# A diffusion trunk on one core: the feature-major projections stream 128 context and 512 latent tokens per weight tile, where they streamed 320 and 320

## The chip, the core and the metric

The kernel runs on one core of a Trainium2 chip. The metric is the device time of one execution in microseconds. The engines are named as in the profile: PE is TensorE's matmul (PEld its weight loads), ACT is ScalarE, DVE is VectorE, POOL is GpSimd and SP is SyncE, which here only issues the loads of the weight stream.

## The reference: one step of a two-layer trunk over 640 tokens

There are 128 context tokens and 512 latent tokens with 1024 features. Layer 0 mixes tokens by retention (4 heads, key width 256, value width 512, forward and backward), layer 1 by windowed attention (16 query heads, 4 key heads, width 64). Each mixer is followed by a gated feed-forward part whose input projection has 5632 outputs and is followed by a convolution of width 3 along the tokens. Context and latent tokens share all weights, but they have their own modulation, and the convolution does not cross from one to the other:

```
def conv_ffn(h, w_in, conv_w, conv_b, w_out):
    a = h @ w_in
    ap = jnp.pad(a, ((0, 0), (1, 1), (0, 0)))
    a = ap[:, :L] * conv_w[0] + ap[:, 1:L + 1] * conv_w[1] + ap[:, 2:] * conv_w[2] + conv_b
    u, g = jnp.split(a, 2, axis=-1)
    return (jax.nn.silu(g) * u) @ w_out
...
    xc = xc + mc[5] * conv_ffn(hc, ...)      # context, 128 tokens
    xl = xl + ml[5] * conv_ffn(hl, ...)      # latent, 512 tokens
```

Everything is in float32.

## The kernel before, in words

**Numbers as two parts.** A float32 operand of a large projection is split into a high part and the rest, both of type fp32r (`w_h`, `w_l` for weights, `h_h`, `h_l` for the normalised tokens, `m_h`, `m_l` for the feed-forward's middle, `y_h`, `y_l` for retention's output). A product is three matmuls, high by high, low by high and high by low, which add up in one PSUM bank. Each matmul instruction brings its own load of the 128x128 stationary operand.

**Weights.** SP streams chunks of 128x1024 into four raw slots. ACT writes `w_h` of a chunk (line 717) and POOL `w_l` (line 1009) into a ring of two. PE's wait for a chunk stands at the head of each tile (`weights`).

**Three kinds of projection on PE.**

- `feature_tile` (lines 335 and 344): the weight tile is stationary and the tokens move, so that the output is 128 features by 640 tokens. The 640 tokens are more than a PSUM bank of 512 float32 holds, so a tile uses two banks, `banks` and `banks + 1`, with half the tokens each, `HALF` = 320. A tile is 2 halves x 8 slices of the 1024 features x 3 products = 48 matmuls. There are 114 such tiles: 4 for each of 4 heads (queries and keys), 44 in the first projection of each feed-forward, and 10 in attention (queries and keys). In 104 of them (line 344) one half runs through all slices and then the other. In 10 of them (line 335), those with a `norm` argument, the halves alternate within a slice, three matmuls each. Four of those ten are the first after a norm and start each slice when its `h_l` is there; the other six have the same code within a loop.
- `token_chunk` (line 359): the tokens are stationary and 512 (in one place 256) weight columns move.
- `out_proj` (line 383): the weights are stationary and 320 tokens move. It takes its tokens by the slice `lo_hi` too.

**Who reads the banks.** After a feature tile ACT copies it out of PSUM. Context and latent tokens go to different places, because the convolution pads between them and rotary embedding is for latent tokens only. With halves of 320 the first bank holds 128 context tokens and 192 latent ones (`CUT` = 192), so three copies are made: 128, 192 and 320 columns (lines 801 to 803, 896 to 898 and 937 to 944). Then DVE works on the copy (the convolution from line 1291 on). PE's next tile but one into the same banks waits for the last of the copies.

**Order.** All engines run hand-written programs with semaphores. There is no scheduler. PE works through: adaptive-norm weights and first norm, four heads (feature tiles, output projection of the head before, token chunks, scores, retention steps), first feed-forward in three groups, attention, second feed-forward in three groups, final norm.

Of the kernel before, what the change touches and what calls it, by code (L numbers as in the profile page):

```python
# [20 lines left out]
ACT = mybir.ActivationFunctionType  # L21
# [5 lines left out]
NCTX, NLAT = 128, 512  # L27
T = NCTX + NLAT
TT = T // P
HALF = T // 2  # L30
CUT = HALF - NCTX
# [109 lines left out]
def build(nc, dr):  # L141
    with ExitStack() as ctx:
# [6 lines left out]
        ps = ctx.enter_context(nc.psum_tensor("ps", [P, 8, 512], F32))  # L149
# [62 lines left out]
        lat_in = front[:, 0:4 * NLAT].rearrange("p (b t) -> p b t", b=4)  # L212
# [50 lines left out]
        def lo_hi(b):  # L263

            return slice(b * HALF, b * HALF + HALF)
# [12 lines left out]
        def ada_at(b, g, q, i):  # L278
# [2 lines left out]
                return None  # L281
            return 12 + q + 2 * i if g == 0 else 20 + i

        def out_bank(mh, at):

            return (at + 4) % 8 if mh == 0 else at
# [27 lines left out]
        def _(pe):  # L314
# [7 lines left out]
            def feature_tile(b, j, i, banks, free, norm=None):  # L322

                s = weights(b, j, i)
                if norm is not None:
                    free(0)
                    free(1)
                    for k in range(KT):  # L330
                        wait_rest(pe, norm, k)
                        wh, wl = (w[:, s, k * P:(k + 1) * P] for w in (w_h, w_l))
                        for half in range(2):
                            for n, (w, x) in enumerate(((wh, h_h), (wh, h_l), (wl, h_h))):
                                mm = nc.tensor.matmul(ps[:, banks + half, 0:HALF], w, x[:, k, lo_hi(half)],  # L335
                                                      start=(k == 0 and n == 0), stop=(k == KT - 1 and n == 2))
                    mm.then_inc(chunk_done, 1)
                    return
                for half in range(2):
                    free(half)  # L340
                    for k in range(KT):
                        wh, wl = (w[:, s, k * P:(k + 1) * P] for w in (w_h, w_l))
                        for n, (w, x) in enumerate(((wh, h_h), (wh, h_l), (wl, h_h))):
                            mm = nc.tensor.matmul(ps[:, banks + half, 0:HALF], w, x[:, k, lo_hi(half)],  # L344
                                                  start=(k == 0 and n == 0), stop=(k == KT - 1 and n == 2))
                mm.then_inc(chunk_done, 1)

# [274 lines left out]
            b = SEG["att"]  # L622
# [84 lines left out]
        def _(act):  # L707
# [86 lines left out]
            def head(b, h, first_head):  # L794
                for j in range(4):
                    act.wait_ge(chunk_done, b.done(j, h))
                    hi(b, j + 2, h)
                    bank, scale = 2 * (j % 2), 1.0 if j < 2 else DK ** -0.5
                    ctx_to = (qT if j < 2 else kT)[:, j % 2, 0:NCTX]
                    lat = front[:, j * NLAT:(j + 1) * NLAT]  # L800
                    nc.scalar.activation(ctx_to, ps[:, bank, 0:NCTX], ACT.Copy, scale=scale)
                    nc.scalar.activation(lat[:, 0:CUT], ps[:, bank, NCTX:HALF], ACT.Copy, scale=scale)
                    nc.scalar.activation(lat[:, CUT:NLAT], ps[:, bank + 1, 0:HALF], ACT.Copy,  # L803
                                         scale=scale).then_inc(qk_evac, 1)
                    if j == 0:
                        act.dma_start(S[:], dr["state"][h]).then_inc(S_in, 16)
                    if not first_head and j in (1, 2):
                        turn_y(h - 1, (0, 1, 2) if j == 1 else (3, 4))
                j = 4
                if not first_head:  # L810
                    for k in range(4):
                        hi(b, 4 + k + 2, h)
                    j = 8
                for proj in range(3):
                    for kc in range(3):
                        hi(b, j + kc + 2, h)
                    for t in range(TT):
                        if t == TT - 1:
                            act.wait_ge(chunk_done, b.done(j + 3, h))
                        else:  # L820
                            act.wait_ge(tile_done, 12 * h + 4 * proj + t + 1)
                        if proj == 0:
                            if t == 0:
                                act.wait_ge(rope_done, 2 * h + 2)
                            op = nc.scalar.copy(v[:, t, :], ps[:, t, :])
                        else:
                            op = nc.scalar.activation((gf, gb)[proj - 1][:, t, :], ps[:, t, :], ACT.Silu)
                        op.then_inc(tok_evac, 1)
                    hi(b, j + 3 + 2, h)
                    j += 4  # L830
                    if proj == 0:

                        act.wait_ge(scores_done, h + 1)
                        if first_head:
                            act.wait_ge(dec_ready, 1)
                        zf, zb = zeta[:, 0, bass.ds(h, 1)], zeta[:, 1, bass.ds(h, 1)]
                        pair = lambda bank: ps[:, bank, :].rearrange("p (c d) -> p c d", c=2)
                        nc.scalar.activation(kz[:, 0, 0, :], ps[:, 6, P:P + DK], ACT.Copy, scale=zf)
                        nc.scalar.activation(kz[:, 1, 0, :], ps[:, 6, P:P + DK], ACT.Copy, scale=zb)
                        nc.scalar.activation(kz[:, 0, 1:3, :], pair(7), ACT.Copy, scale=zf)  # L840
                        nc.scalar.activation(kz[:, 1, 1, :], ps[:, 7, DK:2 * DK], ACT.Copy, scale=zb)
                        nc.scalar.activation(kz[:, 0, 3, :], ps[:, 4, 0:DK], ACT.Copy, scale=zf)
                        nc.scalar.activation(kz[:, 1, 2:4, :], pair(4), ACT.Copy, scale=zb).then_inc(kz_done, 1)

                for n in range(10):
                    act.drain()
                    act.wait_ge(o_done, 10 * h + n + 1)
                    nc.scalar.activation(junk[:], ps[:, 6 + n % 2, :], ACT.Square,
                                         accum_out=small[:, 64 + n:65 + n]).then_inc(ss_done, 1)
                    if n == 1:  # L850
                        if not first_head:
                            act.wait_ge(st_stored, 32 * h)
                        for d in range(2):
                            act.wait_ge(u_done, 8 * h + d + 1)
                            nc.scalar.copy(st_out[:, d], ps[:, 2 * d:2 * d + 2, :]).then_inc(st_copied, 1)
                        for d in range(2):
                            act.wait_ge(st_copied, 2 * h + d + 1)
                            act.dma_start(dr["new_state"][d, h], st_out[:, d]).then_inc(st_stored, 16)
# [21 lines left out]
            def ffn_phase(l, norm):  # L880
                tiles0 = 0
                for g, tiles in enumerate(GROUPS):
                    b = SEG["in", l, g]
                    pairs = b.mains // 2
                    with act.Fori(0, tiles // pairs) as i:
                        for q in range(pairs):
# [3 lines left out]
                            for w in range(2):  # L890
                                act.wait_ge(chunk_done, b.done(2 * q + w, i))
                                hi(b, 2 * q + w + 2, i)

                                act.wait_ge(conv_done[l], 2 * n + w + 1 + 2 * pairs * i)
                                a = ca[:, par, w]
                                nc.scalar.copy(a[:, 1:1 + NCTX], ps[:, 2 * w, 0:NCTX])
                                nc.scalar.copy(a[:, NCTX + 2:NCTX + 2 + CUT], ps[:, 2 * w, NCTX:HALF])
                                nc.scalar.copy(a[:, NCTX + 2 + CUT:NCTX + 2 + NLAT],  # L898
                                               ps[:, 2 * w + 1, 0:HALF]).then_inc(a_evac[l], 1)
                                if blk is not None and w == 0:  # L900
                                    slot, used = b.chunk(b.ada[(4 * q if g == 0 else 0) + 3], i)
                                    act.wait_ge(raw_used[slot], used)
                                    nc.scalar.copy(ada_o[:, q, :], ps[:, 4 + q, :]).then_inc(ada_copied, 1)
# [24 lines left out]
            for j in range(10):  # L928
# [10 lines left out]
                else:  # L939
                    for r in range(2):  # L940
                        rows = slice(64 * r, 64 * r + 64)
                        nc.scalar.copy(ak[rows, 2 * (j - 8) + r, 0:NCTX], ps[rows, bank, 0:NCTX])
                nc.scalar.copy(lat_in[:, j % 4, 0:CUT], ps[:, bank, NCTX:HALF])
                nc.scalar.copy(lat_in[:, j % 4, CUT:NLAT], ps[:, bank + 1, 0:HALF]).then_inc(aqk_evac, 1)
            hi(b, 12, 0)
            for t in range(TT):
                if t == TT - 1:
# [594 lines left out]
```

## Time and profile before

| | us |
|---|---|
| median of two runs | 2219.54 (2217.85 and 2221.23) |
| span of the profiled execution, the only time given of it | 2220.6 |
| PE busy | 2100.9 (95%) |
| PEld busy | 1833.4 (83%) |
| DVE busy | 920.7 (41%) |
| POOL busy | 665.6 (30%) |
| ACT busy | 634.8 (29%) |

The page lists the busy time of each engine, the span in 40 slices, the chain of work that ended last and the costliest groups of instructions. A matmul's duration in a row is from its start to its modelled end. Matmuls overlap, so that the time from one start to the next, which I call the pace, is shorter: it comes from a stretch of the chain or of the timeline divided by the number of instructions in it. A group's line in the chain counts instructions, and a float32 matmul (not fp32r) appears as two instructions.

### The profile page before, as it was taken

The numbers are of one execution on the slowest core, as the hardware profiler recorded it, in microseconds if no ns is written. First come the engines' busy times: TensorE is split into PE (matmuls) and PEld (weight loads), VectorE is DVE, ScalarE is ACT, GpSimd is POOL, SyncE is SP. The second block draws the span as 40 slices with busy tenths as digits, with TensorE's granted clock in tenths as the row PEclk, the third lists the DMA queues.
The fourth block names the chain that finished last, engine by engine and source line by source line (L and its number), as shares of the span: only waits on it lengthen the run. The fifth ranks groups of instructions, "written<-read, shape, count | busy, mean of one in ns | idle before, by whom it ended". The sixth has DMA issues, their size and how long they took to land.

```text
span 2220.6 us, 32261 instructions
## 1 busy us (share of the span) xinstructions
PE 2100.9 (95%) x12352; PEld 1833.4 (83%) x12352; DVE 920.7 (41%) x1452; ACT 634.8 (29%) x1222; POOL 665.6 (30%) x404
## 2 busy tenths in 40 slices
PE   5799999999999997999999998899989899999997
PEld 3686888598598766899999997885559899999997
DVE  1511420340241036552553363646742764364363
ACT  2323212212222323331232232234432332232232
POOL 1323233233323323233333334330004233333333
PEclk7799999999999997999999998899989899999998
DMA  6422232232133202552343222120001122222221
GB/s 242 165 69 76 95 105 76 95 106 75 58 106 104 94 20 76 176 200 79 110 139 112 73 72 81 49 72 1 1 9 59 48 76 76 76 76 76 73 71 56
DMA packets 52435, 189.94 MB, mean 86 GB/s; under 512 B 5872, under 2 KB 7152, under 8 KB 51696
## 3 DMA queue, kind: packets, MB, share of 16 engines
q1 hardware_dynamic: 47232, 171.99, 24.0%
q10 hardware_dynamic: 5104, 16.53, 1.9%
q8 instruction: 75, 1.23, 0.2%
q14 instruction: 24, 0.20, 0.0%
HBM read 181.41 MB, written 7.08 MB: 85 GB/s over the span
## 4 chain that ended last, share of the span: by engine, by line
PE 86%; DVE 5%; issue 2%; ACT 1%; POOLq 1%; DMA 1%; POOL 1%; DVEq 1%; ACTq 0%; SPq 0%
PE ps L344 33%; PE ps L383 20%; PE ps L359 16%; PE ps L335 2%; PE ps L399 2%; PE ps L684 2%; PE ps L528 2%; PE ps L537 1%; PE ps L650 1%; DVE front L1120 1%; POOLq L1035 1%; PE ps L667 1%; DVE front L1115 1%; PE ps L523 1%; PE ps L419 1%
## 5 line engine op out<-in xcount | busy, mean ns | idle before, releaser
L1009 POOL TENSOR_TENSOR w_l<-raw,w_h 128x1024 fp32r<-128x1024 f32 x232 | 560.7, 2417 | 1362.4 <-ACT w_h L717 1361.9
L344 PE MATMUL ps<-h_h,w_h 128*128 128x320 f32 x1664 | 518.3, 311 | 2.0 <-issue 2.0
L344 PE MATMUL ps<-h_l,w_h 128*128 128x320 f32 x1664 | 514.9, 309 | 0.0
L344 PE MATMUL ps<-h_h,w_l 128*128 128x320 f32 x1664 | 514.8, 309 | 0.0
L717 ACT CAST w_h<-raw 128x1024 fp32r<-128x1024 f32 x232 | 243.3, 1049 | 930.3 <-PE ps L383 307.5
L344 PEld LDWEIGHTS ps<-h_h,w_h 128*128 128x128 f32 x1664 | 313.2, 188 | 17.3 <-issue 17.3
L344 PEld LDWEIGHTS ps<-h_l,w_h 128*128 128x128 f32 x1664 | 313.1, 188 | 0.2 <-issue 0.2
L344 PEld LDWEIGHTS ps<-h_h,w_l 128*128 128x128 f32 x1664 | 313.0, 188 | 0.0
L1291 DVE TENSOR_SCALAR cc<-ca,vec 128x641 f32<-128x641 f32 x88 | 165.1, 1876 | 181.8 <-ACT ca L898 181.4
L1155 DVE SCALAR_TENSOR_TENSOR xT<-ps,mods,xT 128x128 f32<-128x128 f32 (+2 forms) x264 | 107.9, 437 | 305.7 <-PE ps L383 305.7
L383 PE MATMUL ps<-m_h,w_h 128*128 128x320 f32 x704 | 217.9, 310 | 2.3 <-DVE mods L1141 2.3
L383 PE MATMUL ps<-m_h,w_l 128*128 128x320 f32 x704 | 217.7, 309 | 0.0
L383 PE MATMUL ps<-m_l,w_h 128*128 128x320 f32 x704 | 217.7, 309 | 0.0
L359 PE MATMUL ps<-w_h,h_h 128*128 128x512 f32 (+1 forms) x520 | 200.2, 385 | 4.9 <-ACT front L803 4.9
L359 PE MATMUL ps<-w_h,h_l 128*128 128x512 f32 (+1 forms) x520 | 198.9, 383 | 0.0
L359 PE MATMUL ps<-w_l,h_h 128*128 128x512 f32 (+1 forms) x520 | 198.8, 382 | 0.0
L383 PEld LDWEIGHTS ps<-m_h,w_h 128*128 128x128 f32 x704 | 132.6, 188 | 2.5 <-DVE mods L1141 2.5
L383 PEld LDWEIGHTS ps<-m_l,w_h 128*128 128x128 f32 x704 | 132.7, 189 | 0.0
L383 PEld LDWEIGHTS ps<-m_h,w_l 128*128 128x128 f32 x704 | 132.6, 188 | 0.0
L359 PEld LDWEIGHTS ps<-w_h,h_h 128*128 128x128 f32 x520 | 98.3, 189 | 26.7 <-ACT front L803 5.8
L359 PEld LDWEIGHTS ps<-w_h,h_l 128*128 128x128 f32 x520 | 98.2, 189 | 19.1
L359 PEld LDWEIGHTS ps<-w_l,h_h 128*128 128x128 f32 x520 | 98.3, 189 | 18.6
(187 smaller groups left out, 2853.2 us busy)
## 6 DMA issues: line engine op xcount, KB each, us to landing
raw<-stream_dram SPq DMA_DIRECT2D x328, 512.0 KB, 3.5
S<-state_dram ACTq DMA_DIRECT2D x4, 1024.0 KB, 7.0
new_state_dram<-st_out ACTq DMA_DIRECT2D x8, 512.0 KB, 3.8
xT<-x_dram ACTq DMA_DIRECT2D x1, 2560.0 KB, 11.7
y_dram<-aq ACTq DMA_DIRECT2D x8, 320.0 KB, 2.4
dm<-diff_dram ACTq DMA_DIRECT2D x1, 512.0 KB, 4.1
rope_t<-rope_t_dram ACTq DMA_DIRECT2D x1, 512.0 KB, 6.7
rope_a<-rope_a_dram ACTq DMA_DIRECT2D x1, 512.0 KB, 3.5
```

The source lines that it names most:

```text
L335: mm = nc.tensor.matmul(ps[:, banks + half, 0:HALF], w, x[:, k, lo_hi(half)], start=(k == 0 and n == 0), stop=(k == KT - 1 and n == 2))
L344: mm = nc.tensor.matmul(ps[:, banks + half, 0:HALF], w, x[:, k, lo_hi(half)], start=(k == 0 and n == 0), stop=(k == KT - 1 and n == 2))
L359: mm = nc.tensor.matmul(ps[:, bank(t), 0:n_cols], x[:, k, t * P:(t + 1) * P], w, start=(k == 0 and n == 0), stop=(k == KT - 1 and n == 2))
L383: mm = nc.tensor.matmul(ps[:, bank, 0:HALF], w, x[:, k, lo_hi(half)], start=(k == 0 and n == 0), stop=(k == tiles - 1 and n == 2))
L399: mm = nc.tensor.matmul(ps[32 * g:32 * g + 32, 4 + par, :], csil[:, k, :], raw[:, s, kk * 512:(kk + 1) * 512], start=(k < 4), stop=(k >= 4))
L419: mm = nc.tensor.matmul(ms_ps[:, t:t + 1], src[:, t * P:(t + 1) * P], ones[:, 0:1], start=(k == KT - 3), stop=(k == KT - 1))
L528: mm = nc.tensor.matmul(ps[:, 6 + d, :], q[:, t, c * P:(c + 1) * P], S[:, d, t, :], start=False, stop=(t == 1))
L684: mm = nc.tensor.matmul(ps[64 * (kv % 2):64 * (kv % 2) + 64, 7, :], val[:, kv * HD:(kv + 1) * HD], pT[:, u % 2, kb, :], start=(kb == 0), s ...
L717: nc.scalar.copy(w_h[:, r, :], raw[:, s, :]).then_inc(hi_ready[r], 1)
L1009: nc.gpsimd.tensor_tensor(w_l[:, r, :], raw[:, s, :], w_h[:, r, :].bitcast(F32), ALU.subtract).then_inc(raw_used[s], 1)
L1155: op = V.scalar_tensor_tensor(out=xT[:, m, tok], in0=ps[:, bank, cols], scalar=mods[:, l, 8 * gate + m, s:s + 1], in1=xT[:, m, tok], op0=A ...
L1291: V.tensor_scalar(c, a[:, 1:1 + CONV], tap[1], tap[3], ALU.mult, ALU.add)
```

## The change

The slice of tokens that a feature tile's two halves take is no longer 0 to 320 and 320 to 640, but 0 to 128 (the context) and 128 to 640 (the latent tokens). The number of matmuls, their order, their weights and the banks stay; each pair of 320 columns becomes one matmul of 128 columns and one of 512. ACT's copies fall from three per tile to two, of 128 and 512 columns. `token_chunk` and `out_proj` are untouched.

```diff
+        def ctx_lat(b):
+
+            return (slice(0, NCTX), slice(NCTX, T))[b]
...
                         for half in range(2):
                             for n, (w, x) in enumerate(((wh, h_h), (wh, h_l), (wl, h_h))):
-                                mm = nc.tensor.matmul(ps[:, banks + half, 0:HALF], w, x[:, k, lo_hi(half)],
+                                mm = nc.tensor.matmul(ps[:, banks + half, 0:(NCTX, NLAT)[half]], w,
+                                                      x[:, k, ctx_lat(half)],
                                                       start=(k == 0 and n == 0), stop=(k == KT - 1 and n == 2))
...
                         for n, (w, x) in enumerate(((wh, h_h), (wh, h_l), (wl, h_h))):
-                            mm = nc.tensor.matmul(ps[:, banks + half, 0:HALF], w, x[:, k, lo_hi(half)],
+                            mm = nc.tensor.matmul(ps[:, banks + half, 0:(NCTX, NLAT)[half]], w,
+                                                  x[:, k, ctx_lat(half)],
                                                   start=(k == 0 and n == 0), stop=(k == KT - 1 and n == 2))
...
                     nc.scalar.activation(ctx_to, ps[:, bank, 0:NCTX], ACT.Copy, scale=scale)
-                    nc.scalar.activation(lat[:, 0:CUT], ps[:, bank, NCTX:HALF], ACT.Copy, scale=scale)
-                    nc.scalar.activation(lat[:, CUT:NLAT], ps[:, bank + 1, 0:HALF], ACT.Copy,
-                                         scale=scale).then_inc(qk_evac, 1)
+                    nc.scalar.activation(lat, ps[:, bank + 1, :], ACT.Copy, scale=scale).then_inc(qk_evac, 1)
...
                                 nc.scalar.copy(a[:, 1:1 + NCTX], ps[:, 2 * w, 0:NCTX])
-                                nc.scalar.copy(a[:, NCTX + 2:NCTX + 2 + CUT], ps[:, 2 * w, NCTX:HALF])
-                                nc.scalar.copy(a[:, NCTX + 2 + CUT:NCTX + 2 + NLAT],
-                                               ps[:, 2 * w + 1, 0:HALF]).then_inc(a_evac[l], 1)
+                                nc.scalar.copy(a[:, NCTX + 2:NCTX + 2 + NLAT], ps[:, 2 * w + 1, :]).then_inc(a_evac[l], 1)
...
-                nc.scalar.copy(lat_in[:, j % 4, 0:CUT], ps[:, bank, NCTX:HALF])
-                nc.scalar.copy(lat_in[:, j % 4, CUT:NLAT], ps[:, bank + 1, 0:HALF]).then_inc(aqk_evac, 1)
+                nc.scalar.copy(lat_in[:, j % 4, :], ps[:, bank + 1, :]).then_inc(aqk_evac, 1)
```

## Rows read from the trace of the kernel before

**Rows 1.** The page: span, busy time and granted clock.

```profile
span 2220.6 us, 32261 instructions
...
PE 2100.9 (95%) x12352; PEld 1833.4 (83%) x12352; DVE 920.7 (41%) x1452; ACT 634.8 (29%) x1222; POOL 665.6 (30%) x404
...
PEclk7799999999999997999999998899989899999998
```

**Rows 2.** The page: the chain that ended last, by engine and by line.

```profile
PE 86%; DVE 5%; issue 2%; ACT 1%; POOLq 1%; DMA 1%; POOL 1%; DVEq 1%; ACTq 0%; SPq 0%
PE ps L344 33%; PE ps L383 20%; PE ps L359 16%; PE ps L335 2%; PE ps L399 2%; PE ps L684 2%; PE ps L528 2%; PE ps L537 1%; PE ps L650 1%; DVE front L1120 1%; POOLq L1035 1%; PE ps L667 1%; DVE front L1115 1%; PE ps L523 1%; PE ps L419 1%
```

**Rows 3.** Chain by time, second feed-forward: start us, us, what xcount.

```profile
1906.52 112.64 PE ps L344 x768
```

**Rows 4.** The same, retention: 512 moving columns.

```profile
144.69 54.45 PE ps L359 x240
```

**Rows 5.** The same, attention's values: 256 moving columns.

```profile
1470.52 14.41 PE ps L359 x120
```

**Rows 6.** PE groups by line and form: xcount | busy us, mean ns.

```profile
L335 PE MATMUL ps<-h_h,w_h 128*128 128x320 f32 x160 | 61.0, 381 | 42.1 <-DVE h_l L1125 36.3 <-POOL h_l L1041 5.7
...
L497 PE MATMUL ps<-qT,kT 128*128 128x128 f32 x80 | 10.0, 280 | 2.8 <-ACT front L825 2.8
```

**Rows 7.** The same on PEld, the weight loads.

```profile
L344 PEld LDWEIGHTS ps<-h_l,w_h 128*128 128x128 f32 x1664 | 313.1, 188 | 0.2 <-issue 0.2
...
L650 PEld LDWEIGHTS ps<-ak,aq 128*128 128x128 f32 x128 | 19.4, 192 | 0.0
...
L425 PEld LDWEIGHTS ps<-front,cst 128*128 128x128 f32 x50 | 11.3, 326 | 8.5 <-DVE front L1098 8.5
...
L656 PEld LDWEIGHTS ps<-maskb,identb 128*128 128x128 bf16 x48 | 4.7, 98 | 7.6 <-issue 7.2
```

**Rows 8.** Timeline of PEld in a norm sum: start us, us, what.

```profile
1372.08 1.42 PEld L419 LDWEIGHTS ps<-cst,front 128*128 128x128 f32 x12
```

**Rows 9.** Timeline of PEld, a little later in the same sum.

```profile
1374.26 1.40 PEld L419 LDWEIGHTS ps<-cst,front 128*128 128x128 f32 x6
```

**Rows 10.** Windows around Rows 8, around Rows 9 and in Rows 3.

```profile
core 0: us, PE busy (x) PEld busy (x) DVE busy (x) ACT busy (x) POOL busy (x), PEclk, DMA share, GB/s
1372.20:1373.40 1.20, 1.20 (x13) 1.20 (x12) 0.00 (x0) 0.00 (x0) 0.00 (x0) 1.00 0.00 0
1374.50:1375.50 1.00, 1.00 (x6) 1.00 (x6) 0.00 (x0) 0.00 (x0) 0.00 (x0) 0.50 0.00 0
1906.50:2019.00 112.50, 112.50 (x770) 112.50 (x769) 66.33 (x67) 37.05 (x75) 38.55 (x16) 1.00 0.23 71
```

**Rows 11.** Timeline of PE, retention's scores: float32, 128 moving columns.

```profile
706.55 1.73 PE L497 MATMUL ps<-qT,kT 128*128 128x128 f32 x14
```

**Rows 12.** Timeline of PE, attention's masks: bf16, 128 moving columns.

```profile
1533.04 0.22 PE L653 MATMUL ps<-maskb,identb 128*128 128x128 bf16 x1
1533.10 0.22 PE L656 MATMUL ps<-maskb,identb 128*128 128x128 bf16 x1
```

**Rows 13.** Timeline of PE in the first feature tile after the first norm.

```profile
65.62 0.47 PE L335 MATMUL ps<-h_l,w_h 128*128 128x320 f32 x1
65.89 0.47 PE L335 MATMUL ps<-h_h,w_l 128*128 128x320 f32 x1
...
69.76 0.63 PE L335 MATMUL ps<-h_h,w_h 128*128 128x320 f32 x1 [0.92 <-DVE h_l L1125]
```

**Rows 14.** Groups on ACT and who waits, on DVE: columns as in Rows 6.

```profile
L898 ACT COPY ca<-ps 128x320 f32<-128x320 f32 x88 | 38.8, 441 | 0.0
...
L897 ACT COPY ca<-ps 128x192 f32<-128x192 f32 x88 | 28.5, 324 | 0.0
...
L984 ACT COPY pT<-ps 128x512 f32<-128x512 f32 x32 | 17.1, 594 | 0.0
...
L1291 DVE TENSOR_SCALAR cc<-ca,vec 128x641 f32<-128x641 f32 x88 | 165.1, 1876 | 181.8 <-ACT ca L898 181.4 <-issue 0.2
```

## The prediction, made before the change was run

> **What bounds the kernel now.** I read the page first. PE is busy for 95% of the span and no other engine for more than 41%, weight loads apart [rows 1]. PE carries 86% of the chain that ended last, and line 344, the feature tile, 33% of it, more than any other line [rows 2]. So what a matmul of a feature tile costs is paid in full, unless PE would have waited there anyway.
>
> The view to read next is the chain in order of time, because a matmul's duration overlaps its neighbour's and only the pace counts. In the second feed-forward 768 matmuls of 320 columns follow each other in one piece of 112.64 us: 146.7 ns each [rows 3]. With 512 moving columns, also fp32r with a load each, the pace is 54.45/240 = 226.9 ns [rows 4], and with 256 it is 14.41/120 = 120.1 ns [rows 5]. All of it is at the full granted clock, 2.4 GHz [rows 1, 10]. The three points lie on one line: (226.9 - 146.7)/192 = 0.418 ns per column, which is a column per clock, and (146.7 - 120.1)/64 = 0.416. What is left is 226.9 - 512/2.4 = 13.6, 13.4 and 13.4 ns per matmul. If nothing else counted, 128 columns would take 53.3 + 13.4 = 66.7 ns, a pair 66.7 + 226.9 = 293.6 ns, and the pair of before is 2 x 146.7 = 293.4 ns. The split would then be free. The question is whether the line goes on below 256 columns.
>
> **Why I think it does not.** Under each matmul lies the load of the next stationary operand, and a shorter matmul hides less of it. The trace shows how fast loads can follow each other when the matmuls are next to nothing. In the norm's sum one column moves per load: twelve loads in 1.42 us [rows 8], of which the last lasts about 0.19 as other float32 loads do [rows 7], so (1.42 - 0.19)/11 = 112 ns each, at a granted clock of 1.00 [rows 10]. These are float32 loads, though. The fp32r loads of the feature tiles last 188 ns in their rows, those of bf16 98, and those of float32 192 [rows 7]. A fp32r load therefore looks like a float32 one and not like a bf16 one. In the scores, float32 with 128 moving columns, fourteen matmuls take 1.73 us [rows 11], the last of them 0.28 [rows 6], so (1.73 - 0.28)/13 = 112 ns. So neither of these two streams of 4-byte loads goes faster than 112 ns at the full clock. The bf16 masks follow each other at 1533.10 - 1533.04 = 0.06 us with 128 columns [rows 12], so it is the load and not the matmul that makes the floor.
>
> The Trainium skill bears on this in two places. The page "TensorE: Matmul & The Clock Gate", section "LDWEIGHTS (loading the stationary operand)", gives the stationary columns over 1.2 GHz, 107 ns for 128; by that the sum below would be 107 us in place of 131, an estimate. The same page's section "Weight-path perf modes — Fast Weight Load (FWL) and DoubleRow" keeps the fast load to types that are not FP32, and the trace agrees as to bf16 against float32 (98 against 192 ns); on which side fp32r stands only the 188 ns say.
>
> **The change, part by part.**
>
> - *Moving columns of the first half, 320 to 128.* Bounds: 112 ns from the float32 loads [rows 8], and 120.1 ns from the nearest row of the same kind of matmul, 256 columns of fp32r [rows 5], if the 13.4 ns come on top of a load of 107 as they come on top of the columns. I take 116, the middle, since each of the rows is like the new matmul in one respect. Against 146.7 that is -30.7 ns. Below 112 I leave 107 as the end, 256 columns' time at a column per clock, since the 256-column matmul hides its load too [rows 5]. Above 120 I leave 140, in case a load can begin only when the matmul before it has begun, and its own matmul waits longer for it than the columns take; the present pace of 147 ns would hide anything up to that.
> - *Moving columns of the second half, 320 to 512.* 226.9 against 146.7 ns: +80.2 ns [rows 3, 4]. Weights are stationary here and tokens in rows 4, but both are 128x128 fp32r against 512 columns of fp32r.
> - *Per tile.* 24 x (-30.7 + 80.2) = 24 x 49.5 ns = 1.19 us. That is 7.04 us (48 x 146.7) grown to 8.23. In the ten tiles whose halves alternate, each 128-column matmul still covers one load, and each 512-column one as well, so the same sum holds.
> - *Tiles in which PE waits anyway.* Line 335 has 42.1 us of idle time before it, nearly all for `h_l` [rows 6]. It lies in four tiles, the first ones after a norm. There a step of two slices takes 69.76 - 65.19 us, that is 4.57, of which PE waits 0.92 [rows 13]. The clock is at half there: the pace is 65.89 - 65.62 = 0.27 us [rows 13], 320 columns at 1.2 GHz. Twelve matmuls become 6 x 0.22 + 6 x 0.43 = 3.9 us in place of 3.2 to 3.65, still under 4.57. The last slice is paid. So 4 x 7/8 = 3.5 tiles are hidden behind DVE's norm, and 110.5 of 114 count. If that cover were gone, it would cost 3.5 x 1.19 = 4 us more.
> - *ACT's copies.* 192 and 320 columns take 324 and 441 ns in their rows, 512 take 594 [rows 14]. Two overlapping starts become one, at most 0.17 us per tile less. DVE waits 181.4 us for these copies in 85 waits [rows 14], but PE doesn't wait for DVE within the phases: the piece of 112.64 us has no gap [rows 3]. Only at the ends of six feed-forward groups is it on the path: under 1 us in all. I put nothing. The wait of PE for the copies (two tiles back) only gets longer cover.
> - *Banks.* PE writes 512 columns into a bank that ACT empties before PE comes back to it a tile later. A longer tile makes this looser. POOL, SP and the DMA queues have the same work and more time for it.
>
> **Sum.** 110.5 x 1.19 = 131 us. The profiled execution's span is 2220.6 us, so I expect a span of 2352. The median of the runs shown is 1.1 us below that span, so the time is **2351 us**. With 107 ns as pace it is 110.5 x 24 x 40.5 ns = 107 us, 2327; with 120.1 it is 110.5 x 24 x 53.6 = 142 us, 2362; with 140 it is 110.5 x 24 x 73.5 = 195 us, 2414.
>
> **The rivals.**
>
> *The load does not bind: not slower.* If a fp32r load can be as quick as bf16's, or two loads can be under way, the line goes on to 66.7 ns and the change costs 0.2 ns per pair: 2220 us. For it: bf16 goes at 60 ns with 128 columns [rows 12], and a 188 ns load beside a 120.1 ns pace [rows 5, 7] shows that loads already overlap. Against it: the 112 ns of rows 8 and of rows 11. The point where it decides: 2% are 44.4 us, 44.4/(110.5 x 24) = 16.7 ns, so a pace under 66.5 + 16.7 = 83 ns is no measurable change. The Trainium skill speaks for this one: "TensorE: Matmul & The Clock Gate", section "Back-to-back issue gap", gives about 81 ns per matmul for a sustained stream of load and matmul pairs at 128 columns, by which the estimate is 38 us, 2258; no row of this trace with 4-byte loads is near 81. I give it 9%, of which 1% for faster.
>
> *A short fp32r matmul loses its single pass.* If 128 columns were handled as float32, a matmul would cost two instructions of 112 ns [rows 11], 223 ns: 24 x (223 - 146.7 + 80.2) = 3.76 us per tile, +415 us, 2635. For it: nothing in the trace shows fp32r below 256 columns. Against it: the line is straight from 512 down to 256 columns [rows 3 to 5], with no sign of a threshold. 7%.
>
> *The clock falls.* Within the first half of a tile the array would work 53 of 116 ns for 2.8 us. In the norm's sum, with one column per load, the granted clock went from 1.00 to 0.50 after some 2 us, and the loads then follow at (1.40 - 0.33)/5 = 214 ns [rows 8 to 10], if the last lasts 0.33 as line 425's do [rows 7]. Every tenth of the tiles' 909 us of work that ran at half clock would add 91 us: 2442, and half of it some 2800. Against it: there the array had next to no columns, while here 128 of them move and 5.4 us of full work follow in every tile, and attention has streams of 128 columns at clock 9 of the page's digits [rows 1]. 6%.
>
> **The numbers.** The forecast has 78%, the four cases together 100%. The range runs from the 107 ns end to the 140 ns end, 2325 to 2415, and holds the forecast's 78% and the mildest part of the falling clock, some 2%. Two per cent, about what a measurement tells from no change here, are 44 us. Faster by that: 1%; within: 8%; slower: 91%, all the rest.
>
> **What would show it.** In the profile after: the pace of 128-column stretches of line 349 (24 in a row) near 116 ns, each 24 in 2.8 us; of 512 columns 227 ns; tiles of 8.2 us in the chain, 16 tiles in 132 us where 112.64 stood; PEld durations near 190 in both; the other two kinds of projection at their old pace; and the granted clock in 40 slices as before, stretched. A pace of 67 ns proves the first rival, of about 220 the second, and digits of 5 to 8 in the feed-forward's slices the third. The forecast is wrong also if a PE wait appears between tiles, which I see no source for.

## The result: 2351.4 us, 5.9% slower

The changed kernel takes 2351.4 us (2350.35 and 2352.45), against 2219.54 before. The ratio is 1.0588 with a 95% interval of 1.057 to 1.0605. The profiled execution's span is 2350.7 us, 130.1 more than before.

The page after, first its span, busy times and granted clock, then who made up the chain. The line numbers move by a few: 344 is now 349, 335 is 339, 383 is 389.

```profile
span 2350.7 us, 32147 instructions
...
PE 2238.0 (95%) x12352; PEld 1849.2 (79%) x12352; DVE 922.3 (39%) x1452; ACT 628.3 (27%) x1108; POOL 658.9 (28%) x404
...
PEclk7799999999999989999999997999987999999998
```

```profile
PE 88%; DVE 4%; issue 2%; ACT 1%; POOLq 1%; POOL 1%; DMA 1%; DVEq 1%; ACTq 0%; SPq 0%
PE ps L349 37%; PE ps L389 19%; PE ps L365 15%; PE ps L339 3%; PE ps L405 2%; PE ps L690 2%; PE ps L534 2%; PE ps L543 1%; PE ps L656 1%; DVE front L1121 1%; POOLq L1036 1%; PE ps L673 1%; PE ps L425 1%; PE ps L529 1%; DVE front L1116 1%
```

Against [rows 1] PE is busy 137 us more, and the other engines as before within 7 us (PEld 16). Against [rows 2] the feature tile's share grew from 33% to 37% and the other projections kept their time (19% of 2351 is 20% of 2221). The digits of the granted clock are the same kind of row, stretched.

The chain in order of time says what a tile costs now. The columns are start in us, us, and what, with the number of instructions.

```profile
239.60 8.14 PE ps L349 x48
...
432.55 10.00 PE ps L349 x48
...
1820.25 28.09 PE ps L349 x144
...
1856.55 24.54 PE ps L349 x144
...
1946.60 56.32 PE ps L389 x384
2002.92 130.85 PE ps L349 x768
```

The piece of 16 tiles that took 112.64 us [rows 3] takes 130.85: 8.18 us per tile in place of 7.04. The output projection beside it has 56.32/384 = 146.7 ns as before the change. The first piece is the first tile of head 1, the second the same tile of head 2, and the two pieces of x144 are three tiles each near the start of the second feed-forward. I come back to these four.

How the tile divides is read from PE's timeline, one row per matmul.

```profile
2100.88 0.22 PE L349 MATMUL ps<-h_h,w_h 128*128 128x128 f32 x1
2100.94 0.28 PE L349 MATMUL ps<-h_l,w_h 128*128 128x128 f32 x1
2101.05 0.27 PE L349 MATMUL ps<-h_h,w_l 128*128 128x128 f32 x1
...
2103.40 0.28 PE L349 MATMUL ps<-h_h,w_l 128*128 128x128 f32 x1
2103.51 0.45 PE L349 MATMUL ps<-h_h,w_h 128*128 128x512 f32 x1
2103.80 0.40 PE L349 MATMUL ps<-h_l,w_h 128*128 128x512 f32 x1
2104.04 0.40 PE L349 MATMUL ps<-h_h,w_l 128*128 128x512 f32 x1
...
2106.34 0.39 PE L349 MATMUL ps<-h_h,w_h 128*128 128x512 f32 x1
2106.57 0.39 PE L349 MATMUL ps<-h_l,w_h 128*128 128x512 f32 x1
```

From 2101.05 to 2103.40 there are 21 steps of 128 columns: 112 ns each. A fp32r matmul of 128 columns after another thus goes at the pace of the float32 loads of [rows 8], and 45 ns slower than its columns and 13.4 ns would take. From 2106.34 on, 512 columns take 0.23 us as in [rows 4]. Two things at the seams are worth seeing. The first short matmul is followed after 0.06 us, and the first long one makes up for it and is followed only after 0.29 us. Together they take 0.35 us, and 112 + 227 = 339 ns is what a short and a long one cost elsewhere: nothing is gained. Why the two records divide the time so unevenly is not shown. And the long matmuls after the seam take 0.24 and 0.23 us; in the trace it is some ten of them at 232 ns on average, until the 227 ns are back. That lag is 0.05 us per tile.

By groups, PE's two forms of line 349 and the wait before the first tiles:

```profile
L349 PE MATMUL ps<-h_h,w_h 128*128 128x512 f32 x832 | 333.4, 401 | 0.0
...
L349 PE MATMUL ps<-h_l,w_h 128*128 128x128 f32 x832 | 230.3, 277 | 0.0
...
L339 PE MATMUL ps<-h_h,w_h 128*128 128x128 f32 x80 | 22.9, 286 | 36.1 <-DVE h_l L1126 31.4 <-POOL h_l L1042 4.7
```

and the loads, on PEld:

```profile
L349 PEld LDWEIGHTS ps<-h_l,w_h 128*128 128x128 f32 x1664 | 318.6, 191 | 33.2 <-issue 0.2
...
L389 PEld LDWEIGHTS ps<-m_l,w_h 128*128 128x128 f32 x704 | 132.0, 187 | 0.2
```

A fp32r load now lasts 191 ns on average where the feature tiles had 188 [rows 7], and 187 still under 320 columns. The load durations alone tell next to nothing of the change; it is the pace that tells.

ACT's copy of 512 columns, and DVE's wait for it:

```profile
L901 ACT COPY ca<-ps 128x512 f32<-128x512 f32 x88 | 52.0, 591 | 0.0
...
L1292 DVE TENSOR_SCALAR cc<-ca,vec 128x641 f32<-128x641 f32 x88 | 166.5, 1892 | 276.1 <-ACT ca L901 276.1
```

DVE waits 276.1 us for ACT where it waited 181.4 [rows 14]. That is 95 us more waiting on an engine off the path: PE delivers later. The chain's stretch of 16 tiles has no wait of PE for DVE in it.

### The profile page after: what moved, and what is told of

Same layout as the page of the kernel before. It is cut to its first block, busy times and chain, and to the rows that moved or that the text cites. A ratio compares the mean times of both kernels' runs of the same rounds, so it can differ in the third digit from the quotient of the medians.

```text
span 2350.7 us, 32147 instructions
## 1 busy us (share of the span) xinstructions
PE 2238.0 (95%) x12352; PEld 1849.2 (79%) x12352; DVE 922.3 (39%) x1452; ACT 628.3 (27%) x1108; POOL 658.9 (28%) x404
## 3 DMA queue, kind: packets, MB, share of 16 engines
HBM read 181.41 MB, written 7.08 MB: 80 GB/s over the span
## 4 chain that ended last, share of the span: by engine, by line
PE 88%; DVE 4%; issue 2%; ACT 1%; POOLq 1%; POOL 1%; DMA 1%; DVEq 1%; ACTq 0%; SPq 0%
PE ps L349 37%; PE ps L389 19%; PE ps L365 15%; PE ps L339 3%; PE ps L405 2%; PE ps L690 2%; PE ps L534 2%; PE ps L543 1%; PE ps L656 1%; DVE front L1121 1%; POOLq L1036 1%; PE ps L673 1%; PE ps L425 1%; PE ps L529 1%; DVE front L1116 1%
## 5 line engine op out<-in xcount | busy, mean ns | idle before, releaser
L1010 POOL TENSOR_TENSOR w_l<-raw,w_h 128x1024 fp32r<-128x1024 f32 x232 | 554.2, 2389 | 1497.1 <-ACT w_h L723 1496.6
L349 PE MATMUL ps<-h_h,w_h 128*128 128x128 f32 (+1 forms) x1664 | 561.2, 337 | 2.2 <-issue 2.2
L349 PE MATMUL ps<-h_h,w_l 128*128 128x128 f32 (+1 forms) x1664 | 557.2, 335 | 0.0
L349 PE MATMUL ps<-h_l,w_h 128*128 128x128 f32 (+1 forms) x1664 | 555.9, 334 | 0.0
L349 PEld LDWEIGHTS ps<-h_h,w_h 128*128 128x128 f32 x1664 | 318.5, 191 | 50.0 <-issue 17.7
L349 PEld LDWEIGHTS ps<-h_h,w_l 128*128 128x128 f32 x1664 | 318.2, 191 | 35.4
L349 PEld LDWEIGHTS ps<-h_l,w_h 128*128 128x128 f32 x1664 | 318.6, 191 | 33.2 <-issue 0.2
L1292 DVE TENSOR_SCALAR cc<-ca,vec 128x641 f32<-128x641 f32 x88 | 166.5, 1892 | 276.1 <-ACT ca L901 276.1
```

Of the source, the lines that this page charges most:

```text
L349: mm = nc.tensor.matmul(ps[:, banks + half, 0:(NCTX, NLAT)[half]], w, x[:, k, ctx_lat(half)], start=(k == 0 and n == 0), stop=(k == KT - 1 ...
L1010: nc.gpsimd.tensor_tensor(w_l[:, r, :], raw[:, s, :], w_h[:, r, :].bitcast(F32), ALU.subtract).then_inc(raw_used[s], 1)
L1292: V.tensor_scalar(c, a[:, 1:1 + CONV], tap[1], tap[3], ALU.mult, ALU.add)
```

## The experiments

Each kernel was run beside the kernel before, and ratios are against that. Where I give a time per tile, it is the piece of 16 tiles in the second feed-forward, divided by 16; the pieces stand in fences of one row each.

### Where the floor begins: 256, 240 and 192 columns first

All three are the kernel before with another cut (the diffs are shortened throughout):

```diff
-CUT = HALF - NCTX
+FIRST = 256   # or 240, or 192
+CUT = FIRST - NCTX
...
-  ps[:, banks + half, 0:HALF], w, x[:, k, lo_hi(half)]
+  ps[:, banks + half, 0:(FIRST, T - FIRST)[half]], w, x[:, k, f_half(half)]
```

> The tiles stream 256 and 384 tokens. Load floor (a matmul's pace is the longer of its columns at 2.4 GHz plus 13.4 ns and 112 ns for the next load): 120.1 + 173.4 = 293.5 ns per pair against 293.4 before, so 2220 us, no change. Rival, short fp32r matmuls (below 256 columns) stream at two clocks per column: 256 is not below, also 2220.

Measured: 2221.5 us, ratio 0.9995 (0.9985 to 1.0005).

```profile
1907.48 112.54 PE ps L349 x768
```

7.03 us per tile, as before the change. An uneven split costs nothing as long as both parts are long enough.

> 240 and 400 tokens. Load floor: 240/2.4 + 13.4 = 113.4 ns, just above 112, and 180.1: 293.5 per pair, so 2220 us, no change. Rival, two clocks per column below 256 columns: 200 + 5 ns for 240 columns, +92 ns per pair in 24 x 110.5 pairs, +243 us, 2463.

Measured: 2227.5 us, ratio 1.0026 (1.0014 to 1.0039).

```profile
1903.54 113.29 PE ps L349 x768
```

7.08 us per tile. Two clocks per column below 256 would have been 2463, so that rival is gone. The 5 us are more than expected: in the trace the 240-column matmuls go at 112 ns, but the 400-column ones take 183.4 and not 180.1.

> 192 and 448 tokens. Load floor: 112 + 200.1 = 312.1 ns per pair, +18.7, +50 us, 2270. Two clocks per column: 165 + 200.1, +72 ns, +190 us, 2410. No floor at all: 2220.

Measured: 2279.0 us, ratio 1.0251 (1.0234 to 1.0268).

```profile
1949.03 120.74 PE ps L349 x768
```

7.55 us per tile; the 192-column matmuls come every 112 to 113 ns, the same as 128 columns and as 240. That is the floor. The 9 us above my figure are again in the long matmul: the 24 of a tile take 203.6 ns on average where the line gives 200.1, 3.5 ns in 2652 pairs. Part of that is the seam, where the first takes 226; the last eleven take 202.3.

### Half the columns at the floor

```diff
-            return (slice(0, NCTX), slice(NCTX, T))[b]
+            return (slice(0, NCTX // 2), slice(NCTX, T))[b]
...
-  ps[:, banks + half, 0:(NCTX, NLAT)[half]]
+  ps[:, banks + half, 0:(NCTX // 2, NLAT)[half]]
```

> The changed kernel, but only 64 of the 128 context tokens are multiplied in the feature tiles, and ACT copies these 64 columns twice. Load floor: the 64-column matmuls stay at 112 ns although the columns are halved, 2351 us as with 128. Two clocks per column: 58 ns in place of 112, -54 ns in 2652 pairs, 2208 us. A floor from the columns alone would show the same gain.

Measured: 2367.9 us, ratio 1.0649 (1.0632 to 1.0667). Chain piece, and a group on PE by line and form:

```profile
2022.43 130.32 PE ps L354 x768
```

```profile
L354 PE MATMUL ps<-h_l,w_h 128*128 128x64 f32 x832 | 232.7, 280 | 0.0
```

8.15 us per tile against 8.18: with half the columns the short matmul is as dear as with 128, so the floor is not a matter of columns. But the kernel is 16 us slower than the changed one, and this was in no expectation. The granted clock shows where:

```profile
PEclk7799999999999978999999998999987899999998
```

The mean granted clock is 0.950 against 0.961, that is 2 x 0.050 x 2367 = 237 us at half clock in place of 2 x 0.039 x 2351 = 183. PE stands idle no longer than before (109 us in place of 113), and in the tiles of the first feed-forward, after 892 us, the granted clock is at half in six stretches of 3.4 us where the profile of the changed kernel has none. The chain has the price of one: such a tile takes 9.88 us where the changed kernel's takes 8.28, so six are some 10 of the 16 us. These are single profiled executions, and the number of columns is not the whole of it. The profile of latent_first, below, has 128 columns and two such stretches in the same phase (tiles of 9.81 and 9.78 us). All eight of these tiles begin right behind eight matmuls that move two columns each (at 909.88 us here, at 898.71 in latent_first), as do tiles that keep the full clock. My third rival, the falling clock, is thus real in a mild form. With 64 columns it came more often, and all four times of this kernel (2362 to 2369) lie above all those of the kernels with 128 fp32r columns (2343 to 2354).

### A quick load in the same place

```diff
+def top(ap):
+    return ap.bitcast(BF16).rearrange("p (n two) -> p n two", two=2)[:, :, 1]
...
+                            if half == 0:
+                                w_, x_ = top(w_), top(x_)
```

> The changed kernel, but the context matmuls of the feature tiles read the upper two bytes of weights and tokens as bf16 (less precise; everything else as in the changed kernel). Load floor: the bf16 loads are quick (98 ns in their rows, pace 56 to 60 ns in attention), so the 128-column matmuls go from 112 to about 60 ns, -52 ns in 2652 pairs, -138 us: 2213. If the 112 ns were a cost of 128 moving columns as such, or if a load with a step of two elements is as slow as a 4-byte one: 2351.

Measured: 2207.5 us, ratio 0.9936 (0.992 to 0.9952). Chain piece, timeline of PE, and loads on PEld:

```profile
1893.11 110.93 PE ps L359 x768
```

```profile
1900.01 0.22 PE L359 MATMUL ps<-h_h,w_l 128*128 128x128 bf16 x1
...
1900.36 0.22 PE L359 MATMUL ps<-h_h,w_l 128*128 128x128 bf16 x1
```

```profile
L359 PEld LDWEIGHTS ps<-h_l,w_h 128*128 128x128 f32 x832 | 156.6, 188 | 29.8
...
L359 PEld LDWEIGHTS ps<-h_l,w_h 128*128 128x128 bf16 x832 | 81.0, 97 | 0.4 <-issue 0.3
```

From 1900.01 to 1900.36 the six steps take 0.06 us each, 57 to 58 ns in the trace, where the same 128 columns with a 4-byte load took 112. The load lasts 97 ns in place of 188. The number and the order of matmuls, the banks, the copies and the tokens are those of the changed kernel, so the type of the operands is worth 144 us here. The run changes the load and the multiplication together; that the columns multiplied are not what matters follows from context64, where half of them saved nothing.

What these two runs leave is a fixed cost of every 4-byte matmul as such, beside its load. Two rows of the kernel before speak against it:

```profile
30.23 1.08 PE L399 MATMUL ps<-raw,csil 128*32 128x512 f32 x4
...
1509.33 1.48 PE L667 MATMUL ps<-cst,pr 128*128 128x128 f32 x12
```

The first are four float32 matmuls with a stationary operand of only 32 columns, which write four different quarters of the partitions. Each lasts 1.06 us in the trace and all four together 1.08, so they start within 0.02 us. The second are float32 transposes with 128 columns, whose loads last 143 ns on average where the others last 188 to 192. They follow each other every (1.48 - 0.27)/11 = 0.110 us (109 ns in the trace), a little faster than the 112. So a 4-byte matmul has no cost of 112 ns in itself there, and I take the load of 128 stationary columns for what makes it. No run has a fp32r matmul without its load, so for fp32r this last step is argued.

### Can loads be banked under the long matmuls?

```diff
-                        for half in range(2):
-                            for n, (w, x) in enumerate(((wh, h_h), (wh, h_l), (wl, h_h))):
+                        for n, (w, x) in enumerate(((wh, h_h), (wh, h_l), (wl, h_h))):
+                            for half in range(2):
```

> The changed kernel, but the context and the latent matmul of each product follow each other (128, 512, 128, 512) with the same weights, where 24 of one came before 24 of the other. Load floor with one load ahead: every 128-column matmul still covers one whole load, 112 + 227, so 2351 us. Rival, loads can run further ahead and be banked under the 512-column matmuls: the pair falls to 67 + 227 = 294 ns, 2220 us.

Measured: 2343.8 us, ratio 1.0554 (1.0535 to 1.0573). Chain piece and timeline (a row x2 is the short and the long matmul of one product, named by the first's shape):

```profile
431.60 8.45 PE ps L350 x48
...
1816.51 24.49 PE ps L350 x144
...
1995.24 130.57 PE ps L350 x768
```

```profile
1999.86 0.50 PE L350 MATMUL ps<-h_h,w_l 128*128 128x128 f32 x2
2000.20 0.50 PE L350 MATMUL ps<-h_h,w_h 128*128 128x128 f32 x2
```

A pair of 128 and 512 columns comes every 0.34 us, 112 + 227, although a 512-column matmul, which has 115 ns to spare, now stands before every short one. If two loads could run ahead, the pair would have shrunk towards 294 ns, so here only one does. The short matmul's record starts early and the long one's is longer, with the same sum. The kernel is 8 us quicker than the changed one, at intervals 1.0535 to 1.0573 and 1.057 to 1.0605. The lag after the seam is 2 us of it (8.16 against 8.18 us per tile). The profiled execution has the rest at full clock: the first tile of heads 2 and 3 takes 8.45 us where the changed kernel's took 10.00, and the first three tiles of the second feed-forward 24.49 where they took 28.09, together 6.7 us. Whether the order of the matmuls keeps the clock up or chance did is not shown.

### Order of the halves, and ACT's copies

```diff
-                for half in range(2):
-                    free(half)
+                free(0)
+                free(1)
+                for half in (1, 0):
```

> The changed kernel, but the 24 latent matmuls of a tile come before its 24 context ones. Same paces. If the half-clock windows that the changed kernel's profile shows in the first tile of heads 2 and 3 (435.0 and 629.6 us, tiles of 9.6 in place of 8.3 us) come from 128-column matmuls right behind PE's wait, they go: 3 to 6 us less, 2346. If they come from the wait alone: 2351.

Measured: 2347.5 us, ratio 1.0563 (1.0547 to 1.0578). The interval overlaps that of the changed kernel, so a gain of 4 us is not shown. The half-clock stretches in the first tiles of heads 2 and 3 are gone in its profile, but others lie elsewhere, and three_copies, with the order of the changed kernel, has none in the heads either. So the order alone doesn't decide whether one falls there. This one is open.

```diff
-                    nc.scalar.activation(lat, ps[:, bank + 1, :], ACT.Copy, scale=scale).then_inc(qk_evac, 1)
+                    nc.scalar.activation(lat[:, 0:CUT], ps[:, bank + 1, 0:CUT], ACT.Copy, scale=scale)
+                    nc.scalar.activation(lat[:, CUT:NLAT], ps[:, bank + 1, CUT:NLAT], ACT.Copy,
+                                         scale=scale).then_inc(qk_evac, 1)
```

> The changed kernel, but ACT copies each tile in three pieces (128, 192, 320 columns) as before the change. The copies are hidden: 2351 us, less than 2 us of difference. If ACT's copies were on the path, their 0.06 to 0.17 us in 114 tiles would show as 7 to 19 us more.

Measured: 2348.5 us, ratio 1.0574 (1.0553 to 1.0596), not slower than with two copies. The saved copy is worth nothing here.

### Using it: bf16 for the cross products

The cross products multiply a high part with a rest, so their lower bits weigh little. If a bf16 matmul is cheaper, they are the place for it. All four kernels here leave out the lower bits of the cross products.

```diff
+def as_used(n, *aps):
+    return aps if n == 0 else [top(ap) for ap in aps]
...
-  w, x[:, k, lo_hi(half)],
+  *as_used(n, w, x[:, k, lo_hi(half)]),
```

> The changed kernel, but in the feature tiles the two cross products (high by low, low by high) read the upper two bytes of both operands as bf16, which leaves out their lower bits. If the load for the next matmul is what each matmul covers, three 128-column matmuls cost 67 (fp32r columns over a bf16 load) + 57 + 112 (bf16 columns over the next fp32r load) = 236 ns in place of 336, and three of 512 columns 227 + 217 + 217 = 661 in place of 681: 120 ns less in 884 triples, -106 us, 2245. If each matmul paid for its own load instead, it would be 112 + 57 + 57 = 226, 2236; if the floor were the columns' own, no gain in the 128s, 2333.

Measured: 2281.3 us, ratio 1.0273 (1.0251 to 1.0295), between 2245 and 2333 and near neither.

```profile
1953.62 121.39 PE ps L359 x768
```

> The kernel before (320 and 320 tokens) with the same cross products as bf16 in the feature tiles. A bf16 matmul costs its columns and 4 ns where a fp32r one costs 13.4, and 137 ns still cover a load of 112: 147 + 137 + 137 = 421 in place of 440 ns, in 2 x 884 triples, -34 us: 2187. If the 13.4 ns belong to the 4-byte load and not to the fp32r matmul, only two of three change as well, but shifted by one: the same 2187. If they belong to every matmul of 320 columns: 2220.

Measured: 2240.5 us, ratio 1.0089 (1.0075 to 1.0103): slower, where I expected 34 us less. Chain piece and timeline:

```profile
1917.15 114.35 PE ps L354 x768
```

```profile
1960.02 0.32 PE L354 MATMUL ps<-h_l,w_h 128*128 128x320 bf16 x1
1960.18 0.30 PE L354 MATMUL ps<-h_h,w_l 128*128 128x320 bf16 x1
1960.21 0.42 PE L354 MATMUL ps<-h_h,w_h 128*128 128x320 f32 x1
1960.47 0.32 PE L354 MATMUL ps<-h_l,w_h 128*128 128x320 bf16 x1
```

A triple takes 1960.47 - 1960.02 = 0.45 us, where three fp32r matmuls take 0.44. The trace has 156, 26 and 265 ns. The bf16 matmul before the fp32r one is followed at once, and the fp32r one by its successor after 265 ns: 26 + 265 = 291 ns for two, and 156 for the first bf16 one. I had priced each type by its pure stream and the change between them at nothing; it costs some 26 ns per triple with 320 columns against my 421, or 20 against the 427 that the last run's 140 ns per bf16 matmul give. Seven ns in 1768 triples are 12 of the 20 us lost; the other 8 I can't place. In cross_split the trace has 247 ns for the 128 columns (236 expected) and 702 for the 512 (661 expected).

> The same in all projections of the kernel before (output projections and token chunks too). There are 1088 more triples of 320 columns and 520 of 512 or 256: 19 ns each, -31 us more: 2156. Faster than both kernels. If PE becomes so quick that a weight chunk is late (ACT and POOL need 3.5 us for a chunk that PE uses 6.7 us), less.

Measured: 2249.6 us, ratio 1.0139 (1.0123 to 1.0155). It was expected at 2156, and it is 9 us slower than cross_even. The other projections lose too, but not alike: the chain has 57.18 us for 384 matmuls of the output projection (7 ns more per triple of 320 columns) and 56.18 for 240 of `token_chunk` (22 ns more per triple of 512), and the 256-column ones stay at 14.42 us for 120.

So the last run sorts by type within each half, so that the type changes once per half.

```diff
+                    high = [(k, 0) for k in range(KT)]
+                    cross = [(k, n) for k in range(KT) for n in (1, 2)]
+                    turn = high + cross if half == 0 else cross + high
+                    for at, (k, n) in enumerate(turn):
```

> The kernel before (320 and 320 tokens); in the 104 tiles of line 344 the cross products are bf16 as in cross_even, but each half runs its 8 high-by-high matmuls in one block and its 16 cross products in another, so that the type changes once per half and not twice per triple. cross_even's triples took 447 ns in its profile, 26 more than 147 + 137 + 137; if those 26 ns are the price of the two changes of type, a tile now costs 16 x 146.7 + 32 x 137.3 + 2 x 13 to 26 ns = 6.77 to 6.79 us in place of 7.04, -26 to -28 us: 2193, faster than both kernels. If a bf16 matmul of 320 columns saves nothing in itself: 2220 or above.

Measured: 2205.2 us, ratio 0.9921 (0.9903 to 0.9939), faster than both kernels, by less than forecast. Chain piece and timeline:

```profile
1895.01 109.54 PE ps L356 x768
```

```profile
1903.44 0.30 PE L356 MATMUL ps<-h_l,w_h 128*128 128x320 bf16 x1
...
1904.28 0.30 PE L356 MATMUL ps<-h_l,w_h 128*128 128x320 bf16 x1
```

A bf16 matmul of 320 columns has a pace of (1904.28 - 1903.44)/6 = 140 ns, not the 137 I had carried over from 128 columns, and a tile takes 6.85 us, not 6.78. What the change under study costs is not won back by this: it is the even split that this version keeps.

## Why the prediction was right, step by step

**What bounds the kernel** held. PE had 95% before and has 95% now, and what a tile costs more stands in the time: summed over all 114 tiles, each from its first matmul's start to its last one's end, the two traces differ by 131.4 us, and the spans by 130.1.

**The pace of 128 columns**, 116 ns, was the step that carried everything, and it was a middle between two rows, chosen because neither could be preferred. The float32 loads' row [rows 8] was the right one: 112 ns. The 256-column row [rows 5] is 120.1 because of its own columns and not because of a load with 13.4 ns on top: 240 and 192 columns go at 112 ns. That is -4 ns x 2652 = -11 us on the sum. The ends of 107 and 140 ns were not needed.

**The pace of 512 columns** was right at 227 ns, but I missed the seam: a tile is 8.18 us and not 24 x (112 + 226.9) = 8.13. That is +5 us.

**The clock.** I gave a falling clock 6% as a case of its own. It came in a mild form on top of the forecast. The windows of the first tile of heads 2 and 3 after the change, and of the second feed-forward's first ordinary tile:

```profile
core 0: us, PE busy (x) PEld busy (x) DVE busy (x) ACT busy (x) POOL busy (x), PEclk, DMA share, GB/s
432.50:442.50 10.00, 9.95 (x51) 8.38 (x51) 1.48 (x3) 0.00 (x0) 0.82 (x3) 0.83 0.01 2
627.50:637.50 10.00, 10.00 (x52) 8.47 (x56) 1.44 (x2) 0.00 (x0) 0.74 (x2) 0.83 0.01 2
1820.20:1831.80 11.60, 11.60 (x49) 10.33 (x48) 4.04 (x4) 1.70 (x3) 2.36 (x1) 0.68 0.15 45
```

and the same tiles of the kernel before (head 2 and the second feed-forward):

```profile
424.60:431.60 7.00, 6.96 (x47) 6.96 (x48) 1.72 (x3) 0.00 (x0) 1.00 (x3) 1.00 0.01 2
1743.60:1751.50 7.90, 7.90 (x50) 7.90 (x49) 4.50 (x5) 1.76 (x4) 2.40 (x1) 0.87 0.18 66
```

The granted clock was 0.83 in the first tile of heads 2 and 3, where it had been 1.00, and 0.68 where it had been 0.87. In the chain above the tile takes 10.00 us in place of 8.14, twice nearly alike, and the start of the second feed-forward 28.09 - 24.54 = 3.6 us more than three ordinary tiles. In the chain of the kernel before that start was only 1.0 us longer than three ordinary tiles, 22.12 against 21.12. That is +2.6 us. The first tile of heads 2 and 3 was already longer than that of head 1 before the change (7.30 against 7.04 us, at full clock), so their half clock is 1.6 us each, +3.2. Against that, the first nine ordinary tiles of attention had a half-clock stretch before (63.98 us in place of 63.4) and none after (73.57), -0.7. While the clock was at half, the short matmuls came every 0.21 us (1820.37 to 1824.85, 21 steps), as the loads of [rows 9] did. In heads 2 and 3 the tile lies behind a wait of PE of 1.0 us and begins with 24 short matmuls. Whether these bring the half clock on is not shown: three_copies has the same order and a wait of 0.9 us there, and full clock. With 64 columns the profile had more half clock, 237 in place of 183 us.

**The sum.** 131.3 - 10.6 + 4.9 + 3.2 + 2.6 - 0.7 = 130.7 against 130.1 measured. That the forecast of 2351 met 2351.4 to within a microsecond is luck: the short matmul's pace was 11 us too dear, the seam and the clock, which were not in the sum, cost 5 us each, and they cancelled. What was right without luck is the path, the 227 ns and that 4-byte loads hold the short matmul near 112 ns.

**Tiles in which PE waits anyway.** The four tiles behind a norm grew, from the first matmul's start to the last one's end, by 1.3 us in all, where four ordinary ones grew by 4 x 1.14 = 4.6. So some 3 us were hidden; I had 4. The wait before line 339 fell by more, from 42.1 [rows 6] to 36.1 us, and part of these tiles runs at half clock, where the longer matmuls cost twice as much; the split between the two is not worked out.

**ACT's copies** at nothing: three_copies agrees. POOL, SP and DMA had no part.

**The rivals.** That the load does not bind is refuted by the changed kernel itself (112 ns and not 67), by split192 and by context64, and the banking of loads by alternate; split256 and split240 fit both. That a short fp32r matmul takes two instructions of 112 ns is refuted by the 112 ns as well. The figure of about 81 ns for a stream of load and matmul pairs with 128 columns, which the Trainium skill gives in "TensorE: Matmul & The Clock Gate", section "Back-to-back issue gap", is met by no 4-byte stream here with 128 stationary columns (109 to 112 ns) and by no bf16 one with 128 columns (57 ns). The same page's 107 ns in "LDWEIGHTS (loading the stationary operand)" is 5 ns below the fp32r and float32 streams of every run and 2 ns below the float32 transposes. A threshold at 256 columns is refuted by split240 and split192. In short: the pace of a fp32r matmul with its own load is the longer of 112 ns and its columns at 2.4 GHz with 13.4 ns (16 to 17 with 400 and 448 columns), and the two meet, by this line, at (112 - 13.4) x 2.4 = 237 columns.

## What to carry to other kernels

When every matmul brings a new stationary tile, look for the pace of the loads alone, in a row where next to nothing moves. A piece whose columns take less time than a load pays for columns that it doesn't have. An even split of tokens over two PSUM banks can be worth more than a tidy one that follows the data. And where types are mixed to save passes or loads, run each type in blocks: a change of type within a triple cost more than the cheaper type saved.

## What the runs showed that I had not expected

- A change between bf16 and fp32r matmuls costs: triples of one fp32r and two bf16 took 447 ns with 320 columns, where 147 + 2 x 140 = 427 would be the pure streams' sum, and the same triples all in fp32r take 440.
- fp32r matmuls of 400 and 448 columns take 183.4 and (away from the seam) 202.3 ns, 3.3 and 2.3 above the line through 256, 320 and 512.
- Behind a run of 24 short matmuls some ten of the 512-column ones take 232 ns and not 227 (0.05 us per tile), also where the short ones are bf16 at 57 ns (bf16_context). Why is not shown.
- With 64 columns in place of 128 the profile had 54 us more at half clock and the kernel took 16 us more time, with no more idle time on PE (109 against 113 us).
